# The down weights of experts 1 to 28 in one transfer each, with even and odd gate and up features in the two column halves

## The reference, cut to what matters

```
logits = xt @ w_router + b_router;  top-4 of 32, softmax -> gates (256, 32)
for each expert:                       # wgu (1024, 2048), wd (1024, 1024)
    hgu  = xt @ wgu + bgu
    gate = min(hgu[:, :1024], 7);  up = clip(hgu[:, 1024:], -7, 7)
    y    = ((up + 1) * (gate * sigmoid(1.702 * gate))) @ wd + bd
    acc += gates[:, e] * y
out = RMSNorm_final(h + acc)
```

## Time and profile before

| | us |
|---|---|
| median of 3 runs | 1162.32 (1161.65 to 1162.6) |
| profiled execution, its own time | 1162.85 |
| its span, first to last instruction | 1161.1 |
| start of the expert part in the span | 243 |
| TensorE busy in the span | 1094.7 (94%) |
| DMA queue of SP: bytes, share of 16 engines | 435.18 MB, 89.3% |

### The profile page before, as it was taken

One profiled execution on the slowest core, in us unless ns is written; L12 is line 12 of the kernel. 1 busy time (PEld: TensorE's weight loads), 2 busy tenths in 40 slices (PEclk: granted clock), 3 DMA queues, 4 the chain that ended last, 5 costly groups with the idle time before them and its releaser, 6 DMA issues.

```text
span 1161.1 us, 14713 instructions
## 1 busy us (share of the span) xinstructions
PE 1094.7 (94%) x6238; PEld 496.1 (43%) x6238; DVE 204.2 (18%) x434; ACT 153.0 (13%) x327; POOL 27.8 (2%) x71
## 2 busy tenths in 40 slices
PE   8999999989999999999999999999999999999986
PEld 7677888443333333333333333433323333334322
DVE  2312213123111111111111111111111111111112
ACT  2254222230000000000000000000000000000002
POOL 0010000210000000000000000000000000000000
PEclk9999999988999999999999999999999998999999
DMA  9962527378999999999999999999999999999995
GB/s 329 338 254 73 214 86 282 147 297 359 426 430 428 430 427 431 432 432 428 432 428 426 424 431 427 430 431 430 431 431 430 431 431 431 430 431 428 427 428 233
DMA packets 37006, 437.27 MB, mean 377 GB/s; under 512 B 4280, under 2 KB 5360, under 8 KB 18576
## 3 DMA queue, kind: packets, MB, share of 16 engines
q1 hardware_dynamic: 35056, 435.18, 89.3%
q10 hardware_dynamic: 1920, 1.65, 0.5%
HBM read 435.76 MB, written 1.06 MB: 376 GB/s over the span
## 4 chain that ended last, share of the span: by engine, by line
PE 56%; DMA 42%; DVE 1%; SPq 1%; issue 0%; ACT 0%; POOL 0%; DVEq 0%; POOLq 0%
DMA ring<-in_w_down_dram 26%; PE bank L1309 18%; DMA ring<-in_w_gate_up_dram 15%; PE bank L1337 12%; PE bank L1090 9%; PE bank L1188 2%; PE bank L1200 2%; PE bank L1093 2%; PE bank L1287 2%; PE bank L1277 2%; PE bank L1328 1%; DMA ring<-in_w_in_dram 1%; PE bank L1322 0%; PE bank L1299 0%; PE bank L1158 0%
## 5 line engine op out<-in xcount | busy, mean ns | idle before, releaser
L1309 PE MATMUL bank<-ring,gates 128*64 128x512 f32 x2048 | 478.4, 610 | 23.9 <-DMA ring<-in_w_gate_up_dram 23.8
L1309 PEld LDWEIGHTS bank<-ring,gates 128*64 128x64 f32 x2048 | 140.6, 139 | 275.1 <-issue 235.5
L1337 PE MATMUL bank<-ring,gates 128*64 128x512 f32 x1024 | 228.4, 594 | 26.2 <-DMA ring<-in_w_down_dram 24.7
L962 DVE TENSOR_SCALAR gates<-bank 128x512 f32<-128x512 f32 x32 | 22.1, 691 | 737.5 <-PE bank L1309 737.5
L1337 PEld LDWEIGHTS bank<-ring,gates 128*64 128x64 f32 x1024 | 72.5, 137 | 176.4 <-issue 135.1
L1090 PE MATMUL bank<-ring 128*128 128x256 f32 x384 | 85.0, 381 | 0.0
L1090 PEld LDWEIGHTS bank<-ring 128*128 128x128 f32 x384 | 72.3, 190 | 11.3 <-issue 1.3
L1277 PEld LDWEIGHTS bank<-onehot,qkT 128*128 128x128 bf16 x1488 | 52.2, 118 | 25.2 <-issue 25.2
L1287 PE MATMUL bank<-gates,scatter_w 64*128 64x512 f32 x248 | 61.6, 615 | 0.0
L702 ACT ACTIVATE gates<-gates 128x512 f32<-128x512 f32 x32 | 20.2, 630 | 287.8 <-DVE gates L962 287.8
L1277 PE MATMUL bank<-onehot,qkT 128*128 128x64 bf16 x1488 | 55.5, 198 | 0.0
(11 more groups left out here) (184 smaller groups left out, 522.1 us busy)
## 6 DMA issues: line engine op xcount, KB each, us to landing
ring<-in_w_gate_up_dram SPq DMA_DIRECT2D x50, 4096.0 KB, 25.5
ring<-in_w_down_dram SPq DMA_DIRECT2D x63, 2048.0 KB, 21.1
ring<-in_w_gate_up_dram SPq DMA_DIRECT2D x28, 2048.0 KB, 11.7
ring<-in_w_in_dram SPq DMA_DIRECT2D x9, 2048.0 KB, 21.3
ring<-in_w_out_dram SPq DMA_DIRECT2D x1, 4096.0 KB, 12.8
ring<-in_w_in_dram SPq DMA_DIRECT2D x4, 512.0 KB, 7.1
ring<-in_w_proj_sb_dram SPq DMA_DIRECT2D x1, 2048.0 KB, 9.1
ring<-in_w_proj_moba_dram SPq DMA_DIRECT2D x1, 2048.0 KB, 7.8
```

The costliest lines, as they stand in the source:

```text
L962: V.tensor_scalar(gate_t, bank[4][:, :], SWIGLU_LIMIT, None, ALU.min).then_inc(gate_rd, 1)
L1309: ins = mm(bank[4 + i][SLOTS * c:SLOTS * (c + 1), :], xeT[:, k, :], ring[:, base + k // 2, n0:n0 + CH], start=False, stop=k == KD - 1)
L1337: ins = mm(bank[6][SLOTS * c:SLOTS * (c + 1), :], rows, ring[:, place, j * D + c * CH:j * D + (c + 1) * CH], start=k == 0, stop=k == KD - 1)
```

## The change

Each expert's down weights are now read as `(o p r) n` with r = 8, so a partition gets 8 neighbouring rows, 32 KiB in one run, over both down slots. For experts 1 to 28 one DMA of 4096 KB does it. It waits until both slots are free, and all of it counts up the semaphore of slot 8. Experts 0, 29 and 30 still load by the half, and 31 in three pieces; each piece then takes 16 KiB (or 8 KiB) out of each 32 KiB run.

With r = 8, partition p holds the rows of features 8p to 8p+7. For the transposed hidden rows to fit, the two column halves now take even (c = 0) and odd (c = 1) features of gate and up: the moving operand of the gate-and-up matmuls, and of their bias rows, has a step of 2 elements. The transpose itself stays as it is; the down product takes block k from `hT[:, k // 2]`, half k % 2. The products, their number and their sizes are unchanged.

```diff
-            dn = w_down[0].rearrange("e (s p r) n -> e s p (r n)", p=P, r=4)
+            dn = w_down[0].rearrange("e (o p r) n -> e o p (r n)", p=P, r=8)
...
-                sp.dma_start(ring[:, DN0 + q, :], rows_of(dn, e, q)).then_inc(slot_in[DN0 + q], 16)
+                sp.dma_start(ring[:, DN0 + q, :], rows_of(dn, e, 0)[:, q * SLOT:(q + 1) * SLOT]).then_inc(slot_in[DN0 + q], 16)
...
+            def load_down_wide(e, done):
+                sp.wait_ge(dn_used, (e + done) * DN)
+                sp.dma_start(flat(DN0, DN0 + 2), rows_of(dn, e, 0)).then_inc(slot_in[DN0], 16)
...
                 with sp.Fori(1, TURN) as i:
                     load_gate_up_wide(i * 2 + 3, GU, done)
-                    load_down(i * 2 + 1, done)
+                    load_down_wide(i * 2 + 1, done)
                     load_gate_up_wide(i * 2 + 4, 0, done)
-                    load_down(i * 2 + 2, done)
+                    load_down_wide(i * 2 + 2, done)
...
                 load_gate_up_wide(TURN * 2 + 3, GU, done, range(0, 1))
-                load_down(TURN * 2 + 1, done)
+                load_down_wide(TURN * 2 + 1, done)
                 load_gate_up_wide(TURN * 2 + 3, GU, done, range(1, 2))
-                load_down(TURN * 2 + 2, done)
+                load_down_wide(TURN * 2 + 2, done)
...
                             mm(bank[4 + i][SLOTS * c:SLOTS * (c + 1), :], expert_sel[:, :],
-                               bgu[:, i * D + c * CH:i * D + (c + 1) * CH], start=True, stop=False)
+                               bgu[:, i * D + c:i * D + c + D - 1:2], start=True, stop=False)
...
-                            n0 = (k % 2) * 2 * D + i * D + c * CH
+                            n0 = (k % 2) * 2 * D + i * D + c
                             ins = mm(bank[4 + i][SLOTS * c:SLOTS * (c + 1), :], xeT[:, k, :],
-                                     ring[:, base + k // 2, n0:n0 + CH], start=False, stop=k == KD - 1)
+                                     ring[:, base + k // 2, n0:n0 + D - 1:2], start=False, stop=k == KD - 1)
...
-                    rows = hT[:, j, SLOTS * s:SLOTS * s + SLOTS]
+                    rows = hT[:, k // 2, SLOTS * (k % 2):SLOTS * (k % 2) + SLOTS]
...
-            def down(g, uses, ss=range(DN)):
+            def down(g, uses, ss=range(DN), odd=None):
                 pe.wait_ge(hT_rd, g + 1)
                 for s in ss:
-                    down_rows(s, DN0 + s, range(4), slot_in[DN0 + s], uses).then_inc(dn_used, 1)
+                    ready, count = (slot_in[DN0], uses) if s == 0 or odd is None else (slot_in[DN0 + 1], odd)
+                    down_rows(s, DN0 + s, range(4), ready, count).then_inc(dn_used, 1)
```

More of the change, by code:

```diff
@@ L384, in last_down @@
                 sp.wait_ge(gu_used, (E - 2 + done) * GU + DN)
-                sp.dma_start(ring[:, 0, :], dn[E - 1, 0]).then_inc(last_in[0], 16)
+                sp.dma_start(ring[:, 0, :], dn[E - 1, 0][:, 0:SLOT]).then_inc(last_in[0], 16)
                 for h in range(2):
                     half = slice(h * 2 * D, (h + 1) * 2 * D)
-                    sp.dma_start(ring[:, 1, half], dn[E - 1, 1][:, half]).then_inc(last_in[1 + h], 16)
+                    sp.dma_start(ring[:, 1, half], dn[E - 1, 0][:, SLOT + h * 2 * D:SLOT + (h + 1) * 2 * D]).then_inc(last_in[1 + h], 16)
             def experts(done):
@@ L392, in experts @@
                 load_gate_up(3, GU, done)
-                load_down(1, done)
+                load_down_wide(1, done)
                 load_gate_up_wide(4, 0, done)
-                load_down(2, done)
+                load_down_wide(2, done)
                 with sp.Fori(1, TURN) as i:
                     load_gate_up_wide(i * 2 + 3, GU, done)
-                    load_down(i * 2 + 1, done)
+                    load_down_wide(i * 2 + 1, done)
                     load_gate_up_wide(i * 2 + 4, 0, done)
-                    load_down(i * 2 + 2, done)
+                    load_down_wide(i * 2 + 2, done)
                 load_gate_up_wide(TURN * 2 + 3, GU, done, range(0, 1))
-                load_down(TURN * 2 + 1, done)
+                load_down_wide(TURN * 2 + 1, done)
                 load_gate_up_wide(TURN * 2 + 3, GU, done, range(1, 2))
-                load_down(TURN * 2 + 2, done)
+                load_down_wide(TURN * 2 + 2, done)
                 load_gate_up_wide(TURN * 2 + 4, 0, done)
                 with sp.Fori(TURN + 1, E // 2 - 3) as i:
-                    load_down(i * 2 + 1, done)
+                    load_down_wide(i * 2 + 1, done)
                     load_gate_up_wide(i * 2 + 3, GU, done)
-                    load_down(i * 2 + 2, done)
+                    load_down_wide(i * 2 + 2, done)
                     load_gate_up_wide(i * 2 + 4, 0, done)
-                load_down(E - 5, done)
+                load_down_wide(E - 5, done)
                 load_gate_up(E - 3, GU, done)
-                load_down(E - 4, done)
+                load_down_wide(E - 4, done)
                 load_gate_up(E - 2, 0, done)
@@ L1350, in last_down, with expert @@
                 down_rows(1, 1, range(2, 4), last_in[2], uses).then_inc(dn_used, 1)
-            def expert(g, scatters, more, base, gu_uses, dn_uses, odd=None):
+            def expert(g, scatters, more, base, gu_uses, dn_uses, odd=None, dn_odd=None):
                 gate_up(g, (0, 1), base, gu_uses, odd)
@@ L1367, in expert, with last_expert @@
                     pe.wait_ge(y_rd, g - 1)
-                down(g - 1, dn_uses)
-            def last_expert(g, gu_uses, dn_uses, odd):
+                down(g - 1, dn_uses, range(DN), dn_odd)
+            def last_expert(g, gu_uses, dn_uses, odd, dn_odd):
                 gate_up(g, (0, 1), GU, gu_uses, odd)
@@ L1378, in last_expert @@
                 pe.wait_ge(y_rd, g - 1)
-                down(g - 1, dn_uses, range(0, 1))
+                down(g - 1, dn_uses, range(0, 1), dn_odd)
                 gate_up(g, (4, 5, 6, 7), GU, gu_uses, odd)
                 weight_columns(g)
-                down(g - 1, dn_uses, range(1, DN))
+                down(g - 1, dn_uses, range(1, DN), dn_odd)
                 pe.wait_ge(gT_rd, g + 1)
@@ L1410, in experts @@
                     ins.then_inc(down_bias_ps, 1)
-                expert(done + 1, False, True, GU, gu_before + 1, dn_before + 1, 4 * passes + 1)
+                expert(done + 1, False, True, GU, gu_before + 1, dn_before + 1, 4 * passes + 1, 3 * passes + 1)
                 if r is None:
@@ L1420, in experts @@
                 expert(done + (E - 3), True, True, GU, gu_before + E // 2 - 1, dn_before + (E - 3), 4 * passes + 3)
-                expert(done + (E - 2), True, True, 0, gu_before + E // 2, dn_before + (E - 2), 3 * passes + 3)
-                last_expert(done + (E - 1), gu_before + E // 2, dn_before + (E - 1), 4 * passes + 4)
+                expert(done + (E - 2), True, True, 0, gu_before + E // 2, dn_before + (E - 2), 3 * passes + 3, 3 * passes + 2)
+                last_expert(done + (E - 1), gu_before + E // 2, dn_before + (E - 1), 4 * passes + 4, 3 * passes + 3)
                 last_down(done + (E - 1), passes + 1)
```

## The result

The changed kernel takes 1169.66 us (median of 5, 1167.56 to 1171.86) against 1162.32: a ratio of 1.0066, 95% interval 1.0051 to 1.0081. The forecast was 1165.9. The profiled execution took 1171.55 us, its span 1169.8, 8.7 more than before.

What follows compares the result with a forecast made beforehand. The DMA engines' rate was taken as the bound. A gap of 4.3 us less 1.5 given back afterwards, plus 0.85 for a slow spell, made +3.6 on 1162.32: 1165.9 us; own range 1163.3 to 1169, wider 1159.5 to 1170.

Steps and rivals of the forecast that it cites:

- What bounds the kernel: Experts in flow, 400 to 600 us: DMA rate is the limit, 29.23 us per expert; TensorE needs 26.18.
- Part 1: Down loads of experts 1 to 28: longer runs save 0.10 us per expert, 2.8 us in all.
- Part 2: Down product starts later and frees its slots later; in flow and at the start this costs nothing.
- the cover of 1.2 us: Start, down 1: issued 3.76 us later, it still finds 1.2 us of DMA work queued.
- Part 3: Load order's turn at expert 13: down 14 issued 5.4 us later, 4.3 lost; +2.8 after 1.5 given back.
- The "middle" between 3.3 and 5.4: Late issue of down 14: engines with 2.1 us left lose 3.3, idle ones 5.4; 4.3 taken.
- Part 4: TensorE's two waits for down weights become one of 2.9 us, which may bring a spell at 1.2 GHz.
- the 0.85 us of this term: Step 13: a slow spell costing 1.7 us of TensorE, at chance one half, adds 0.85 us.
- Part 5: Gate and up matmuls: the step of 2 in the moving operand costs nothing.
- rival D: Gate and up matmuls: step costs 0.09 us per pair, 2.9 us per step; 1171 us, chance 0.08.
- the prediction's own signs: Gate and up matmuls stay at 592 to 610 ns, a step without waits at 26.2 us; more refutes the free step.
- E: Down loads: packets don't get longer or cost the same, so gap without gain; 1168.7 us, chance 0.07.

Runs made afterwards that it cites:

- one_dma_16k: Kernel before, but one DMA and one wait for both down halves of experts 1 to 28, still in 16 KiB runs: 1169.61 us, ratio 1.0071.
- layout_only: Changed kernel with its new rows and step of 2, but every down half loaded and waited for by itself: 1163.88 us, ratio 1.0010.
- wide_halves_at_turn: Changed kernel, but down 12 to 14 by halves; experts 13 to 16 load half of gate/up, down, other half: 1161.58 us, ratio 0.9995.
- wide_no_step: Changed kernel, but gate, up and bias rows read by halves without a step (another sum of the same size): 1169.04 us, ratio 1.0046.
- no_step_turn_at_19: Changed kernel without the step; down 12 to 14 by halves; experts 13 to 18 load half of gate/up, down, other half: 1162.96 us, ratio 1.0018.
- before_late_14: Kernel before, but the first half of expert 14's down weights waits for both slots: 1164.09 us, ratio 1.0037.
- before_smooth_turn: Kernel before, but experts 13 to 18 load first half of gate/up, down, second half; down first from 19: 1161.62 us, ratio 0.9993.

## Why the prediction was right, and where it was not

**What bounds the kernel** was right: the DMA engines' rate, and in flow 29.14 us per expert, as the last part of the prediction asked for (29.1 to 29.15).

**Part 1** was right before the turn, in its size (0.09 us per expert for 0.10) and in its cause: one_dma_16k leaves the gain to the length of the runs. Behind the turn it came out smaller: the bytes show 0.6 us over 13 experts, and TensorE's waits are 29.14 us apart against 29.21 before. In sum the gain is 1.5 us in the profile, where 2.8 was the term. The Trainium skill (DMA: Bandwidth & Descriptors, Anatomy of one DMA) puts about 2 us on each DMA, fitted on DMAs that GpSimd issues; with other DMAs queued behind it, one DMA fewer per expert saves 0.01 us at most here (29.22 against 29.23).

**Part 2, the start,** was wrong: cost nothing was the forecast, 3.3 us came in the profiled execution. SP issues down 1 there 5.4 us later than the 289.85 of before, where 3.76 had been counted:

```profile
295.21 0.33 SPq L379 DMA_DIRECT2D ring<-in_w_down_dram  x1
```

layout_only, with narrow loads, issues it at 291.91. So 2.1 us of the 5.4 come from TensorE's stepped matmuls, on whose steps SP's issues hang here, and the cover of 1.2 us had been read with the old steps. The size depends on the clock of the execution. Among those with a granted clock of 0.90 from 256 to 290 us, as before, the loss from 240 to 340 is 3.3 us with wide loads and step (changed, wide_halves_at_turn), 2.3 with the step alone (layout_only) and 0.6 to 0.8 with wide loads alone (wide_no_step, no_step_turn_at_19). So most of it is the step. In the medians the whole kernel lost 7.3 us and not 8.7, and layout_only 0.9; how much of the start is in them is not shown.

**Part 3, the turn,** was the right mechanism, and the place was right to a few us: no transfer after 660, issue of down 14 at 666.12. Its size was forecast as 4.3 and came out as 7.1, in two holes: 1.0 us from 600 to 650 (422 GB/s against 431) and 6.0 from 650 to 720 (386 against 423). Two terms explain the second. The "middle" between 3.3 and 5.4 should have been the upper end: before_late_14 lost 3.7 of 3.8. And step 14 was longer by 0.7, so 5.4 + 0.7 = 6.1. The first is a hole that the prediction didn't see: between the landing of down 12 and the issue of down 13 only the first half of gate and up 15 is queued, 9.7 us of transfer, against 7.1 us of TensorE and the time until a landing is seen and a new DMA moves its first bytes, which no row separates. From 635 to 640 us the share is 0.79. With a slow spell it becomes a hole of some 3 us, as in wide_no_step (184 GB/s from 635 to 640).

**Part 4** was right in kind: single gaps, clocks of 0.96 in 600 to 640 us, and 8.8 us for a down product every second or third expert. The gaps are shorter than the 2.9 us forecast, since the stepped matmuls take 0.7 us of them, and they alternate:

```profile
602.99 8.78 PE L1341 MATMUL bank<-ring,gates 128*64 128x512 f32 x32 [2.06 <-DMA ring<-in_w_down_dram]
...
632.13 7.09 PE L1341 MATMUL bank<-ring,gates 128*64 128x512 f32 x32 [0.35 <-DMA ring<-in_w_down_dram]
```

A slow product ends 1.7 us later, so the next wait is only 0.35 us long, and in this kernel no spell followed such a wait. In the profiled execution the spell fell on step 12 and left step 13 out, so the 0.85 us of this term are not in the 7.1.

**Part 5** was the other wrong term: nothing was taken for the step of 2, and it is (3.75 - 3.58) / 8 = 0.021 us per pair, 0.7 us per step (26.86 us from 639.22 to 666.08, without a wait), a quarter of rival D. (A pair without waits takes 3.58 / 8 = 0.45 us, not quite the 0.43 that the prediction went by.) By the prediction's own signs (592 to 610 ns, a step of 26.2) the 627 ns and 26.86 us speak for a small D. As forecast for D, it costs nothing in flow (29.14 us with the step and, in wide_no_step, without it). The Trainium skill (SBUF — State Buffer, Door 1) has two hits per line of 16 bytes as enough for full bandwidth: the runs show 5% less, so it is nearly so. With one hit per line the rate halves; the same section's remark that 4 float32 can be stepped for free does not hold here, a step of 4 doubles the matmul's time.

The total, +3.6 forecast and +7.3 in the medians, was partly luck. The forecast's own range ended at 1169, and 1169.66 lies above it; only the wider one, to 1170, which was drawn to take in other cases, holds it. The gain was smaller and three costs (start, turn, step) larger than forecast, all in the same direction. By the number alone rivals E (1168.7) and D (1171) were nearer. E is refuted by 29.14 us in flow, and D's price per pair was four times the measured one.

## What to carry to other kernels

A transfer that is made wider moves two dates, not one: it can be used only when all of it has landed, and issued only when all of its room is free. In flow neither cost anything here (29.14 us per expert); the price was paid where the queue of transfers is shortest, so look for that place (where the issuing engine changes its order, and at the start) before the change and count TensorE's whole product behind the landing. Compare the bytes moved by stretch between two traces: it shows in one line per stretch where time went, even if the gain and the loss lie 100 us apart.

## What the runs showed of the hardware

- A moving float32 operand with a step of 8 bytes costs 5% of a paired matmul of 512 columns, with 16 bytes 105% (3.75 and 7.33 us for 16 of them instead of 3.58). With 8 bytes it is the same whether or not the two column halves read the same lines; with 16 bytes only the case where they do was run.
- From 300 us on, a wait of TensorE in one piece of 2.0 to 3.1 us was followed by a spell at 1.2 GHz in 8 of 12 cases in the changed kernel, 4 of 6 before and 11 of 13 in wide_no_step (a down product then takes 8.8 us instead of 7.1, granted clock 0.69 to 0.75 over 5 us). Two waits of 1.2 to 1.4 us per step, as before has them from 419 to 629 us, were followed by none.
- One DMA of 4 MiB instead of two of 2 MiB, with other transfers queued, saves 0.01 us at most; runs of 32 KiB per partition instead of 16 KiB save 0.08 us on 4.19 MB (29.14 against 29.22 us per expert).
- The first column of the table differs by 6 us between executions of nearly the same code. The clock of the first experts goes with it; the stretch of 256 to 290 us, first of the kernel before, then of before_smooth_turn, which is the same there:

```profile
256.00:290.00 34.00, 34.00 (x186) 12.36 (x184) 10.16 (x19) 4.19 (x8) 0.47 (x2) 0.90 0.91 372
```

```profile
256.00:290.00 34.00, 34.00 (x198) 12.95 (x197) 10.95 (x20) 4.39 (x9) 0.47 (x2) 1.00 1.00 415
```

A clock of 0.90 against 1.00, and 372 against 415 GB/s, since the loads there wait for TensorE. This would account for single executions of one kernel that lie 5 us apart (before: 1159.24 to 1164.15 in one group), though only the profiled ones show it; a difference of 1 us needs many executions.
